# Sixteen experts on all tokens, or on tokens sorted into blocks by group

## The chip, the cores and the metric

The kernel runs on one NeuronCore of a Trainium2 chip. Its engines work in parallel and wait for each other through semaphores: PE (TensorE, matmuls; its weight loads are listed apart as PEld), DVE (VectorE), ACT (ScalarE), POOL (GpSimd), and SP, which here only issues DMAs. The metric is the device time of one execution in microseconds (us), lower is better.

## What is computed

Three layers on 256 tokens of width 1024, all in float32. The first two (a gated delta rule beside a dilated attention, then a convolved gated FFN) and the mixer of the third are the same in both kernels. The change is in the end of the third layer, a mixture of experts with two levels of routing:

```
def hier_moe(h, wg, bg, we, be, w_gate, w_up, w_down):     # h = rms_norm(x, ffn_norm_g)
    glog = t @ wg + bg                                      # 4 groups: the best one (top 1)
    ...
    elog_sel = jnp.einsum('tge,tg->te', elog, g_onehot)     # 4 experts of that group: the best two
    ...
    gates = (g_onehot[:, :, None] * w_local[:, None, :]).reshape(T, N_EXPERTS) * p_group
    for e in range(N_EXPERTS):                              # 16 experts, 1024 -> 256 -> 1024
        hid = jax.nn.silu(t @ w_gate[e]) * (t @ w_up[e])
        y = y + gates[:, e:e + 1] * (hid @ w_down[e])
```

A token's gates are zero in all groups but its own, so at most 4 of the 16 experts can matter to it, and 2 do.

## The kernel before, in words

Weights arrive as tiles of 128 partitions x 1024 float32 (512 KB each). To multiply in float32 precision on the fast path, every tile is split into two float32r parts: ACT copies it rounded (`hi`), DVE subtracts that from the tile (`lo`), and PE makes three products for each operand pair, hi\*hi, hi\*lo and lo\*hi (helper `product`, lines 1246 to 1248). All activations are split in the same way.

A ring of 3 raw slots (`ring`) and 3 split slots (`w`) carries the tiles. SP issues the load of tile n+3 when DVE has made `lo` of tile n; ACT makes `hi` of tile n+3 (line 1586) when PE has finished tile n; DVE makes its `lo` (line 1824); PE waits for `lo`. There are 330 tiles in all, 96 of them of the experts.

The mixture of experts begins after the last token sums of `w_out` (PE). DVE adds them to `x` (line 1032), ACT takes squares and a root, DVE scales the rows, PE turns them (line 1327), ACT and DVE split them into `act`, POOL adds the parts again into `h` (line 2142), and PE makes the router's logits from `h` (lines 592, 594) after the first two expert tiles. DVE then works out the gates in short steps on a few columns each (lines 1046 to 1100); PE turns them and spreads each expert's gate over the partitions (line 629), with ACT copying the results (line 807).

Every expert has four up tiles (two of the gate projection, two of the up projection) and two down tiles. With up tiles the weights stand still in PE (128x128) and all 256 tokens move: 8 x 3 matmuls of 256 columns per tile (`project`). With down tiles the hidden values stand still, and the weights move: 2 token halves x 2 column halves x 3 matmuls of 512 columns per tile (`token_product`). Down tiles of expert e come after the up tiles of expert e+1. ACT makes the silu (line 790), DVE the gated up projection (1110) and the product's `hi` (1118), POOL the product and its `lo` (1199, 1203). The experts run in loops on each engine, and the sums over all experts stay in four PSUM banks until the end, when DVE adds them to `x` (line 1142) and SP stores four parts.

## Time and profile before

| | |
|---|---|
| time, median of 3 runs | 1334.0 us (1331.05 to 1336.51) |
| profiled execution, span | 1334.9 us |
| PE / PEld busy | 1263.1 us (95%) / 1168.5 us (88%) |
| DVE / ACT / POOL busy | 817.3 / 663.9 / 328.5 us |
| DMA | 180.98 MB, mean 136 GB/s |
| mixture of experts, from the addition of the mixer's result (1025.6) to the end | 309.3 us |

The profiled execution's span is within 0.1% of the median, so times read from it need no scaling. A busy time is a sum over instructions; PE's matmuls overlap, so that a matmul lasts longer than the distance to the next one. In rows of matmuls the distance between two starts is what one costs when PE is never idle.

### The profile page before, as it was taken

What the parts mean: (1) busy time and instruction counts of PE and PEld (TensorE: products, weight loads), DVE (VectorE), ACT (ScalarE), POOL (GpSimd) and SP (SyncE); (2) the same over time, 40 slices, a digit from 0 to 9 for tenths busy, and PEclk for the clock granted to TensorE, in tenths of its full rate; (3) what the DMA queues carried; (4) which work ended last, traced back from release to release, by engine and by line L of the source; (5) the groups of instructions that cost most, each with busy time, mean ns of one, the idle gap of its engine ahead of it and who ended that gap; (6) DMA issues with size and microseconds to landing.
All of it is one profiled execution on the core that took longest, in us unless ns stands there. A gap on an engine that the chain in (4) does not pass through costs nothing.

```text
span 1334.9 us, 24113 instructions
## 1 busy us (share of the span) xinstructions
PE 1263.1 (95%) x8802; PEld 1168.5 (88%) x8802; DVE 817.3 (61%) x1293; ACT 663.9 (50%) x1085; POOL 328.5 (25%) x370
## 2 busy tenths in 40 slices
PE   8999898999998999899899999888689999999998
PEld 7998787999997999788899998788668889999997
DVE  5766446766666855655766666597455455555554
ACT  6654245655555763345655555583144444444442
POOL 2013300322222101610322222487200122222221
PEclk9999899999999999899899999998659889999999
DMA  6542003565553444103365556233103245665563
GB/s 225 174 144 94 33 1 110 183 188 186 182 185 124 160 146 143 45 1 98 117 190 183 182 186 190 93 127 111 48 1 111 79 144 186 186 186 182 186 186 127
DMA packets 49788, 180.98 MB, mean 136 GB/s; under 512 B 5568, under 2 KB 5728, under 8 KB 49600
## 3 DMA queue, kind: packets, MB, share of 16 engines
q1 hardware_dynamic: 48816, 176.98, 41.8%
q0 software_dynamic: 912, 3.16, 0.7%
q8 instruction: 42, 0.69, 0.2%
q14 instruction: 18, 0.15, 0.0%
HBM read 179.07 MB, written 1.05 MB: 135 GB/s over the span
## 4 chain that ended last, share of the span: by engine, by line
PE 84%; DVE 6%; POOL 4%; ACT 4%; issue 1%; DMA 0%; POOLq 0%; SPq 0%; DVEq 0%; ACTq 0%
PE bank L1246 23%; PE bank L1247 22%; PE bank L1248 22%; PE bank L1481 2%; PE bank L1470 1%; PE bank L1479 1%; PE bank L1305 1%; PE bank L1327 1%; ACT sq L1595 1%; POOL region L1186 1%; PE bank L1296 1%; PE bank L629 1%; POOL region L1161 1%; POOL region L1164 1%; PE bank L1333 1%
## 5 line engine op out<-in xcount | busy, mean ns | idle before, releaser
L1824 DVE TENSOR_TENSOR w<-ring,w 128x1024 fp32r<-128x1024 f32 x330 | 412.2, 1250 | 220.1 <-ACT w L1586 220.1
L1246 PE MATMUL bank<-act,w 128*128 128x256 f32 x1728 | 499.9, 289 | 15.9 <-DVE w L1824 6.1
L1247 PE MATMUL bank<-act,w 128*128 128x256 f32 x1728 | 494.9, 286 | 0.0
L1248 PE MATMUL bank<-act,w 128*128 128x256 f32 x1728 | 494.7, 286 | 0.0
L1586 ACT ACTIVATE w<-ring 128x1024 fp32r<-128x1024 f32 x330 | 347.7, 1055 | 184.6 <-PE bank L1248 180.0
L1246 PEld LDWEIGHTS bank<-act,w 128*128 128x128 f32 x1728 | 337.9, 196 | 23.1 <-issue 15.4
L1247 PEld LDWEIGHTS bank<-act,w 128*128 128x128 f32 x1728 | 337.9, 196 | 2.3
L1248 PEld LDWEIGHTS bank<-act,w 128*128 128x128 f32 x1728 | 337.4, 195 | 0.0
L2094 DVE SCALAR_TENSOR_TENSOR region<-bank,pf,region 128x255 f32<-128x255 f32 (+1 forms) x176 | 84.8, 482 | 77.3 <-ACT region L1787 66.2
L1246 PE MATMUL bank<-w,hid 128*128 128x512 f32 x304 | 119.3, 392 | 4.1 <-POOL hid L2196 2.1
L1247 PE MATMUL bank<-w,hid 128*128 128x512 f32 x304 | 118.9, 391 | 0.0
L1248 PE MATMUL bank<-w,hid 128*128 128x512 f32 x304 | 118.3, 389 | 0.0
L1787 ACT ACTIVATE region<-bank,pf 128x256 f32<-128x256 f32 x88 | 49.6, 564 | 134.3 <-PE bank L1248 134.3
L2193 POOL TENSOR_TENSOR region<-region 128x256 f32<-128x256 f32 x44 | 65.2, 1482 | 183.0 <-DVE region L2094 133.8
L2142 POOL TENSOR_TENSOR h<-act 128x256 f32<-128x256 f32 x48 | 38.5, 841 | 256.7 <-DVE act L1846 256.6
L1246 PE MATMUL bank<-w,act 128*128 128x256 f32 (+1 forms) x208 | 71.7, 345 | 0.0
L1246 PEld LDWEIGHTS bank<-w,hid 128*128 128x128 f32 x304 | 57.3, 188 | 15.6 <-issue 2.9
L1248 PE MATMUL bank<-w,act 128*128 128x256 f32 (+1 forms) x208 | 69.5, 334 | 0.0
L1247 PE MATMUL bank<-w,act 128*128 128x256 f32 (+1 forms) x208 | 69.4, 334 | 0.0
L1248 PEld LDWEIGHTS bank<-w,hid 128*128 128x128 f32 x304 | 57.1, 188 | 12.4
L1247 PEld LDWEIGHTS bank<-w,hid 128*128 128x128 f32 x304 | 57.3, 189 | 9.7
L1199 POOL TENSOR_TENSOR region<-region 128x256 f32<-128x256 f32 x32 | 24.7, 772 | 154.6 <-DVE region L1110 154.6
(329 smaller groups left out, 1656.8 us busy)
## 6 DMA issues: line engine op xcount, KB each, us to landing
ring<-wtiles SPq DMA_DIRECT2D x330, 512.0 KB, 3.6
region<-packp POOLq DMA_DIRECT2D x4, 512.0 KB, 4.3
cst<-consts SPq DMA_DIRECT2D x1, 1348.0 KB, 11.6
x<-xt SPq DMA_DIRECT2D x2, 512.0 KB, 5.9
out<-x SPq DMA_DIRECT2D x4, 256.0 KB, 2.7
pa<-packa POOLq DMA_DIRECT2D x3, 285.5 KB, 4.6
pb<-packb SPq DMA_DIRECT2D x1, 260.5 KB, 11.5
cst<-consts SPq DMA_DIRECT2D x1, 192.5 KB, 2.7
```

The costliest lines, as they stand in the source:

```text
L629: mm = t.matmul(bank[6 + i % 2][:, j * S:(j + 1) * S], ident[0:NE, 2 * i + j:2 * i + j + 1].to_broadcast([NE, P]), gate_t[0:NE, :], start= ...
L1199: pl.tensor_tensor(e_prod[:, j, :], e_act[:, j, :], e_up[:, j, :], ALU.mult).then_inc(ex_prod, 1)
L1246: t.matmul(out_, still[:, 0], moving[:, 0], start=first, stop=False)
L1247: t.matmul(out_, still[:, 0], moving[:, 1], start=False, stop=False)
L1248: return t.matmul(out_, still[:, 1], moving[:, 0], start=False, stop=last)
L1481: mm = t.matmul(bank[6 + g][:, u % 4 * P:u % 4 * P + P], xs[:, u, :], uinv[:, u, :], start=True, stop=True)
L1586: a.activation(w_hi[:, s, :], ring[:, s, :], ACT.Copy).then_inc(hi_ready, 1)
L1787: a.activation(dst[:, q, :], bank[UP_BANKS[2 * q + w]][:, 0:S], ACT.Identity, scale=pf_("conv", p * 6 + w * 3 + 2), bias=pf_("bias", p * 2 ...
L1824: v.tensor_tensor(w_lo[:, s, :], ring[:, s, :], w_hi[:, s, :].bitcast(F32), ALU.subtract).then_inc(lo_ready, 1)
L2094: ins = v.scalar_tensor_tensor(dst[:, q, j:], src[:, 0:S - j], pf_("conv", p * 6 + w * 3 + 2 - j), dst[:, q, j:], ALU.mult, ALU.add)
L2142: pl.tensor_tensor(h[:, k, :], act_hi[:, k, :].bitcast(F32), act_lo[:, k, :].bitcast(F32), ALU.add).then_inc(h_ready, 1)
L2193: pl.tensor_tensor(glu_p[:, q, :], glu_a[:, q, :], glu_v[:, q, :], ALU.mult).then_inc(prod_done, 1)
```

## The change

The experts run on tokens sorted by group. 640 places, five blocks of 128, are filled with the 256 tokens: the largest group gets blocks 0 and 1, the other three one block each; places without a token stay zero. Two one-hot matrices made on the chip do the sorting: `pm` (token x place) gathers the tokens by matmul, its transpose `pmt` adds the results back to the tokens. The gates are gathered with them. The gain `ffn_norm_g` goes into the router's weights and into the splitting of the gathered columns; the norm's factor goes in with the gates, so that the router starts from `x` itself (transposed by PE, line 1707).

The expert weights are in an array of their own, `etiles`. A group's number is read from the counts into a register of SP (`gid`), and the loads of that group's tiles take their address from it. So no expert tile can be loaded before the routing has counted the groups; the loop of loads of `wtiles` ends with the mixer. Raw slots are five (three of `ring`, two in `sq`), split slots seven (three of `w`, four of `wx`).

Per expert there are still four up tiles and two down tiles of the same size. Now the tokens stand still in all of them and the weights move in 512 columns: an up tile holds two slices of 128 rows by 512 columns (gate 256, up 256). An expert of the first (largest) group is applied to two blocks, one of the others to one block. The order of tiles is as before: up tiles of step i+1, down tiles of step i. After the up tiles the hidden values have tokens on partitions, so PE turns them before the down product (`turn_hidden`). POOL makes `lo` of the first down tile of every expert (`POOL_TILE`), DVE of the other five. Loops are written out on all engines. After a group's last expert its sums leave PSUM, are split (`result_hi`, `result_lo`) and scattered to the tokens (`scatter`).

```diff
+BLOCKS = NG + 1
+PLACES = BLOCKS * P
+UPS, DOWNS = 4, 2
+E_TILES = UPS + DOWNS
+RAWS, WEIGHTS = 5, 7
...
+def blocks_of(p):
+    return (0, 1) if p == 0 else (p + 1,)
...
+def tile_order():
+    out = []
+    for i in range(len(STEPS) + 1):
+        if i < len(STEPS):
+            out += [(*STEPS[i], j) for j in range(UPS)]
+        if i >= 1:
+            out += [(*STEPS[i - 1], j) for j in range(UPS, E_TILES)]
+    return out
...
+POOL_TILE = UPS
...
-            keep_warm(14)
-            turn(2 * DEPTH + 1, SECOND_SUMS)
-            first = T2 + U_EXP
...
+            XT_BANKS = (0, 1, 4, 5)
+            for i in range(2 * NT):
+                c, j = divmod(i, 2)
+                pe.wait_ge(*x_half(i + 1))
+                for k in range(KD // 2):
+                    mm = transpose(bank[XT_BANKS[i]][:, k * P:(k + 1) * P],
+                                   x[:, c, (j * KD // 2 + k) * P:(j * KD // 2 + k + 1) * P])
+                mm.then_inc(xt_turned.sem, 1)
+            pe.wait_ge(*consts_ready(2))
             for c in range(NT):
                 for k in range(KD):
-                    t.matmul(bank[5][:, c * NR:(c + 1) * NR], h[:, k, c * P:(c + 1) * P], pb_("wrt", k * NR, NR),
-                             start=k == 0, stop=False)
-                mm = t.matmul(bank[5][:, c * NR:(c + 1) * NR], ones[0:1, :], pb_("rbias", 0, NR, slice(0, 1)),
-                              start=False, stop=True)
-            mm.then_inc(rt_done, 1)
-            def expert_up(n, e, slots, between=None):
-                for j, s in enumerate(slots):
-                    if j == 2 and between:
-                        between()
-                    if j < 2:
-                        pe.wait_ge(ex_act, 2 * e + j - 1)
-                    else:
-                        pe.wait_ge(ex_up, 2 * e + j - 3)
-                    project(n + j, s, bank[j][:, 0:S])
-            def expert_down(n, e, slots, first=False, last=False):
-                pe.wait_ge(ex_hid, 2 * e + 2 + EX_CREDITS)
-                for j, s in enumerate(slots):
-                    tile_in(n + j)
-                    token_product(EXPERT_SUMS, hid_both[:, :, j, :], s, first and j == 0, last and j == 1)
-            for j in range(2, 4):
-                project(first + j, j % SLOTS, bank[j][:, 0:S])
-            def gates_out():
-                pe.wait_ge(gates_ready, 1)
+                    if k % (KD // 2) == 0:
+                        pe.wait_ge(*(xt_act, xt_dve)[c](k // (KD // 2) + 1))
+                    mm = t.matmul(bank[2][:, c * NR:(c + 1) * NR], x_turned[:, c, k, :], pb_("wrt", k * NR, NR),
+                                  start=k == 0, stop=k == KD - 1)
+            mm.then_inc(rt_done.sem, 1)
+            keep_warm(6)
...
+            def gather(out_, k, first, end):
                 for c in range(NT):
-                    mm = transpose(bank[4][0:NE, c * P:(c + 1) * P], r_gate[:, c, :])
-                mm.then_inc(gt_done, 1)
-                pe.wait_ge(gt_ready, 1)
-                for i in range(NE // 2):
-                    if i >= 2:
-                        pe.wait_ge(gbc_ready, i - 1)
+                    for part in range(2):
+                        mm = t.matmul(out_, x_parts[:, part, c, k * P:(k + 1) * P], pm[:, c, first:end],
+                                      start=c == 0 and part == 0, stop=c == NT - 1 and part == 1)
+                mm.then_inc(ga_done.sem, 1)
+            pe.wait_ge(*xs_lo(NT))
+            pe.wait_ge(*pm_ready(1))
+            for k in range(KD):
+                if k >= 4:
+                    pe.wait_ge(*ga_lo(k - 3))
+                gather(bank[4 + k % 4][:, 0:S], k, 0, S)
+            keep_warm(4)
...
+            def expert_up(i):
+                p, e = STEPS[i]
+                for j in range(UPS):
+                    w_ = weights_in(E_AT[(p, e, j)])
+                    if i == 0:
+                        pe.wait_ge(*ga_lo(2 * j + 2))
+                        if j == UPS - 1:
+                            gather_gates()
+                    for n, b in enumerate(blocks_of(p)):
+                        for kk in range(2):
+                            mm = product(bank[n], act_g[:, :, 2 * j + kk, b * P:(b + 1) * P],
+                                         w_[:, :, kk * 512:(kk + 1) * 512], j == 0 and kk == 0, j == UPS - 1 and kk == 1)
+                    mm.then_inc(e_done.sem, 1)
...
+            def expert_down(i):
+                p, e = STEPS[i]
+                pe.wait_ge(*ex_lo(hidden_count(i)))
+                if i == 0:
+                    pe.wait_ge(*ga_lo(2 * KD))
+                    pe.wait_ge(*pt_ready(3))
+                elif e == 0:
+                    pe.wait_ge(*y_lo(finished(p - 1)))
+                for jj in range(DOWNS):
+                    w_ = weights_in(E_AT[(p, e, UPS + jj)])
+                    for n, b in enumerate(blocks_of(p)):
+                        still = hid_both[:, :, hidden_place(i, n), jj * P:(jj + 1) * P]
+                        for j in range(2):
+                            mm = product(acc_bank(p, n, j), still, w_[:, :, j * HALF:(j + 1) * HALF],
+                                         e == 0 and jj == 0, e == NPG - 1 and jj == DOWNS - 1)
+                            if e == NPG - 1 and jj == DOWNS - 1 and (n, j) != (len(blocks_of(p)) - 1, 1):
+                                mm.then_inc(y_done.sem, 1)
+                    mm.then_inc(e_done.sem, 1)
...
+            def turn_hidden(i):
+                p, e = STEPS[i]
+                for n, b in enumerate(blocks_of(p)):
+                    pe.wait_ge(*ex_hid(hidden_count(i - 1) + n + 1))
+                    for jj in range(DOWNS):
+                        mm = transpose(bank[2 + n if p == 0 else 1][:, jj * P:(jj + 1) * P],
+                                       hidv[:, hidden_place(i, n), jj * P:(jj + 1) * P])
+                    mm.then_inc(ht_done.sem, 1)
...
+            for i in range(NE + 1):
+                if i < NE:
+                    expert_up(i)
+                if i == 0:
+                    pe.wait_ge(*pm_ready(2))
+                    for k in range(KD):
...
+                if i >= NPG and (i - 1) % NPG == 0 and i > 1:
+                    p = (i - 1) // NPG - 1
+                    pe.wait_ge(*y_lo(finished(p)))
                     for j in range(2):
-                        mm = t.matmul(bank[6 + i % 2][:, j * S:(j + 1) * S],
-                                      ident[0:NE, 2 * i + j:2 * i + j + 1].to_broadcast([NE, P]), gate_t[0:NE, :],
-                                      start=True, stop=True)
-                    mm.then_inc(gbc_done, 1)
-            expert_up(first + 4, 1, (1, 2, 0, 1), gates_out)
-            expert_down(first + 8, 0, (2, 0), first=True)
-            with pe.Fori(1, NE - 1) as e:
-                expert_up(e * RING + (first + 4), e + 1, (1, 2, 0, 1))
-                expert_down(e * RING + (first + 8), e, (2, 0))
-            expert_down(first + NE * RING - 2, NE - 1, (1, 2), last=True)
+                        scatter(p, j, p == 0, False)
+                if i >= 1:
+                    expert_down(i - 1)
+                if i < NE:
+                    turn_hidden(i)
+            for j in range(2):
+                pe.wait_ge(*y_lo(finished(NG - 2) + j + 1))
+                scatter(NG - 1, j, False, True)
...
+            def weight_hi(n):
+                act.wait_ge(e_in[n % RAWS], 16 * (n // RAWS + 1))
+                if n >= WEIGHTS:
+                    act.wait_ge(*e_done(n - WEIGHTS + 1))
+                a.activation(weight_slot(n)[:, 0], raw_slot(n), ACT.Copy).then_inc(e_hi.sem, 1)
...
+            def silu(i):
+                p, e = STEPS[i]
+                act.wait_ge(*e_done(E_AT[(p, e, UPS - 1)] + 1))
+                if i == 0:
+                    act.wait_ge(*gs_ready(1))
+                for n, b in enumerate(blocks_of(p)):
+                    a.activation(e_act[:, hidden_place(i, n), :], bank[n][:, 0:S], ACT.Silu,
+                                 scale=gs[:, b, 0:1]).then_inc(ex_act.sem, 1)
...
+            def weight_lo(n):
+                dve.wait_ge(*e_hi(n + 1))
+                w_ = weight_slot(n)
+                v.tensor_tensor(w_[:, 1], raw_slot(n), w_[:, 0].bitcast(F32), ALU.subtract).then_inc(e_lo_dve.sem, 1)
...
+            for n in range(len(E_ORDER) + WEIGHTS + 2):
+                if n < len(E_ORDER) and E_ORDER[n][2] != POOL_TILE:
+                    weight_lo(n)
+                if n == 1:
+                    local_gates()
+                    put_places(S, PLACES)
...
+                pl.tensor_tensor(x_parts[:, 1, c, :], x[:, c, :], x_parts[:, 0, c, :].bitcast(F32), ALU.subtract).then_inc(xs_lo.sem, 1)
+            for n, tile in enumerate(E_ORDER):
+                if tile[2] == POOL_TILE:
+                    pool.wait_ge(*e_hi(n + 1))
+                    w_ = weight_slot(n)
+                    pl.tensor_tensor(w_[:, 1], raw_slot(n), w_[:, 0].bitcast(F32), ALU.subtract).then_inc(e_lo_pool.sem, 1)
...
-            with pool.Fori(0, NE) as e:
-                expert(e)
...
+            for n, (p, e, j) in enumerate(E_ORDER):
+                if group[p] is None:
+                    sp.wait_ge(*gid_ready(min(p, 1) + 1))
+                    group[p] = sp.value_load(gid[0:1, p:p + 1], min_val=0, max_val=NG - 1)
+                if n >= RAWS:
+                    if E_ORDER[n - RAWS][2] == POOL_TILE:
+                        sp.wait_ge(*e_lo_pool(split_by(n - RAWS, True)))
+                    else:
+                        sp.wait_ge(*e_lo_dve(split_by(n - RAWS, False)))
+                sp.dma_start(raw_slot(n), etiles[bass.ds(group[p], 1), e * E_TILES + j].rearrange("o p n -> (o p) n")
+                             ).then_inc(e_in[n % RAWS], 16)
```

Three places of the instruction order, as they stand in the program. First, PE from the end of `w_out` on, before: keep_warm is line 1313, the turned rows are `y`, and the expert's first tile follows at once.

```order
L1246 MATMUL bank<-w,act 128x512
L1247 MATMUL bank<-w,act 128x512
L1248 MATMUL bank<-w,act 128x512
L1313 MATMUL bank<-cst 128x128 x14
L1327 MATMUL bank<-cst,y 128x128 x8
L1313 MATMUL bank<-cst 128x128 x4
L1327 MATMUL bank<-cst,y 128x128 x8
L1246 MATMUL bank<-act,w 128x256
```

The same place now (keep_warm is line 1693, the gather line 791, `x` is turned by line 1707):

```order
L1707 MATMUL bank<-cst,x 128x128 x16
L773 MATMUL bank<-pb,h 128x20 x16
L1693 MATMUL bank<-cst 128x128 x6
L780 MATMUL bank<-region,cst 128x4
L781 MATMUL bank<-region,cst 128x4
L782 MATMUL bank<-region 128x4
L783 MATMUL bank<-region,cst 128x4
L784 MATMUL bank<-region 128x4
L1693 MATMUL bank<-cst 128x128 x8
L791 MATMUL bank<-pm,act 128x256 x32
L1693 MATMUL bank<-cst 128x128 x4
L1626 MATMUL bank<-w,act_g 128x512
```

The router, the counts and the gather of the first two blocks have moved ahead of the first expert tile. Second, DVE from the token sums to the first `lo` of an expert's weights, before (1846 splits `act`, 1046 to 1077 are the router's steps):

```order
L1032 TENSOR_TENSOR x<-x,bank 128x1024 x2
L1838 RECIPROCAL x_inv<-x_rms 128x1
L1840 TENSOR_SCALAR y<-x,x_inv 128x1024
...
L1846 SCALAR_TENSOR_TENSOR act<-bank,pb,act 128x256 x8
L1824 TENSOR_TENSOR w<-ring,w 128x1024 x3
L1061 COPY region<-bank 128x40
L1046 TENSOR_REDUCE region<-region 128x2
```

and now (1404 writes `pm`, 1415 splits a gathered slice, 1431 to 1440 work out the experts' scores, 1421 makes `lo` of a weight tile, 1445 begins the gates):

```order
L1404 TENSOR_SCALAR pm<-region 128x256 x2
L1408 SCALAR_TENSOR_TENSOR gid<-cst,region 128x3
L1410 TENSOR_TENSOR region<-region 128x8
L1415 SCALAR_TENSOR_TENSOR act_g<-bank,pb,act_g 128x256 x8
L1431 TENSOR_TENSOR region<-region 128x16 x2
L1433 TENSOR_REDUCE region<-region 128x8
...
L1440 TENSOR_TENSOR region<-region 128x2
L1421 TENSOR_TENSOR w<-ring,w 128x1024 x2
L1445 TENSOR_REDUCE region<-region 128x2
```

The router's first choice, `pm`, the gathered slices and the scores have moved ahead of the first weight tile; the gates stand between the second and the third. Third, DVE in the loop over experts, before (one pass), register instructions left out:

```order
L1824 TENSOR_TENSOR w<-ring,w 128x1024
...
L1110 TENSOR_TENSOR region<-bank,region 128x256
...
L1824 TENSOR_TENSOR w<-ring,w 128x1024
...
L1118 TENSOR_TENSOR hid<-region 128x256 x2
...
L1824 TENSOR_TENSOR w<-ring,w 128x1024
```

and an expert of the second group now, with five tiles on DVE (1471 is the gated product, 1480 the `lo` of the turned hidden values):

```order
L1471 SCALAR_TENSOR_TENSOR mix<-bank,region 128x256
L1421 TENSOR_TENSOR wx<-sq,wx 128x1024
L1480 TENSOR_TENSOR hid<-bank,hid 128x256
L1421 TENSOR_TENSOR wx<-ring,wx 128x1024 x2
L1421 TENSOR_TENSOR w<-ring,w 128x1024
L1421 TENSOR_TENSOR w<-sq,w 128x1024
L1471 SCALAR_TENSOR_TENSOR mix<-bank,region 128x256
```

The number of tiles per expert on DVE went from six to five, the four short instructions to two that read PSUM, and the sixth tile stands in POOL's row of work (`L1572 TENSOR_TENSOR`), where the short products stood.

## Rows read from the trace of the kernel before

**Rows 1.** Windows of the expert part: stretch, length, busy of each engine, PEclk, DMA share, GB/s

```profile
1025.60:1034.20 8.60, 6.43 (x54) 5.92 (x53) 4.77 (x9) 5.05 (x10) 0.03 (x1) 1.00 0.24 74
1034.20:1077.00 42.80, 40.19 (x239) 36.36 (x239) 18.12 (x51) 20.31 (x32) 9.62 (x14) 0.80 0.18 62
1077.00:1317.00 240.00, 240.00 (x1699) 226.59 (x1700) 132.48 (x143) 114.18 (x126) 54.92 (x57) 1.00 0.60 187
1317.00:1334.90 17.90, 12.03 (x55) 9.40 (x54) 6.78 (x10) 2.12 (x2) 2.02 (x3) 1.00 0.20 71
```

**Rows 2.** PE in order of time: start us, us, instruction

```profile
1008.20 0.39 PE L1246 MATMUL bank<-w,act 128*128 128x512 f32 x1
1008.43 0.39 PE L1247 MATMUL bank<-w,act 128*128 128x512 f32 x1
...
1034.43 0.28 PE L1247 MATMUL bank<-act,w 128*128 128x256 f32 x1
1034.55 0.28 PE L1248 MATMUL bank<-act,w 128*128 128x256 f32 x1
...
1040.82 1.96 PE L592 MATMUL bank<-pb,h 128*128 128x20 f32 x16 [0.59 <-POOL h L2142]
```

**Rows 3.** Groups by form, 1075 to 1325 us: count, busy, mean ns, idle before

```profile
L1824 DVE TENSOR_TENSOR w<-ring,w 128x1024 fp32r<-128x1024 f32 x89 | 113.9, 1280 | 94.6 <-ACT w L1586 94.6
L1586 ACT ACTIVATE w<-ring 128x1024 fp32r<-128x1024 f32 x89 | 94.1, 1058 | 98.1 <-PE bank L1248 93.9 <-DMA ring<-wtiles 4.2
L1110 DVE TENSOR_TENSOR region<-bank,region 128x256 f32<-128x256 f32 x30 | 12.8, 426 | 11.9 <-PE bank L1248 11.9
```

**Rows 4.** Groups by form of DVE and POOL, whole span

```profile
L1846 DVE SCALAR_TENSOR_TENSOR act<-bank,pb,act 128x256 fp32r<-128x256 f32 x8 | 3.7, 484 | 2.0 <-ACT act L1606 1.7
L1142 DVE TENSOR_TENSOR x<-x,bank 128x512 f32<-128x512 f32 x4 | 2.7, 687 | 4.9 <-PE bank L1248 4.9
L2171 POOL TENSOR_TENSOR y<-region,cst 128x1024 f32<-128x1024 f32 x12 | 24.8, 2074 | 39.4 <-DVE region L2043 26.5 <-PE bank L1470 12.9
L2196 POOL TENSOR_TENSOR hid<-region,hid 128x256 fp32r<-128x256 f32 x44 | 32.5, 738 | 79.3 <-DVE hid L2104 79.1
```

**Rows 5.** POOL beside DVE, in order of time

```profile
1103.15 2.33 POOL L1203 TENSOR_TENSOR hid<-region,hid 128x256 fp32r<-128x256 f32 x2 [4.65 <-DVE hid L1118]
...
1103.75 1.23 DVE L1824 TENSOR_TENSOR w<-ring,w 128x1024 fp32r<-128x1024 f32 x1 [0.41 <-ACT w L1586]
...
125.39 4.54 POOL L2171 TENSOR_TENSOR y<-region,cst 128x512 f32<-128x512 f32 x3
...
126.51 1.56 DVE L2035 TENSOR_TENSOR region<-cst,y 128x512 f32<-128x512 f32 x1 [0.20 <-POOL y L2171]
```

**Rows 6.** ACT and DVE at the norm and the router, in order of time

```profile
1029.51 1.04 ACT L1595 ACTIVATE sq<-x 128x1024 f32<-128x1024 f32 x1
...
1040.88 1.28 ACT L790 ACT_TABLE_LOAD   x1 [2.84 <-POOL credit L1190]
...
1046.12 0.16 DVE L1046 TENSOR_REDUCE region<-region 128x2 f32<-128x8 f32 x1
1046.32 0.17 DVE L1048 TENSOR_TENSOR region<-region 128x8 f32<-128x8 f32 x1
```

**Rows 7.** DMA issues (the page): KB each, us from issue to landing

```profile
ring<-wtiles SPq DMA_DIRECT2D x330, 512.0 KB, 3.6
out<-x SPq DMA_DIRECT2D x4, 256.0 KB, 2.7
```

**Rows 8.** Windows of the first loads and of two stretches at the lower clock

```profile
6.00:14.00 8.00, 7.43 (x61) 7.24 (x60) 3.08 (x6) 7.57 (x11) 0.00 (x0) 1.00 1.03 424
945.00:1000.00 55.00, 47.30 (x248) 38.49 (x250) 31.40 (x84) 20.73 (x60) 0.00 (x0) 0.56 0.09 29
1062.00:1076.00 14.00, 12.85 (x42) 10.43 (x42) 2.84 (x5) 6.62 (x11) 2.98 (x4) 0.51 0.01 1
1076.00:1080.00 4.00, 3.63 (x31) 3.45 (x30) 3.52 (x4) 1.79 (x2) 1.48 (x1) 1.00 0.46 136
```

533 lines of the change are left out of this document (369 added, 164 removed).

## The prediction, made before the changed kernel was run

> **What bounds the kernel now.** I read the windows of the expert part first, then PE in order of time, then the groups by form of DVE, ACT and POOL with what ended their idle time. From 1077 to 1317 us PE has 240.00 of 240.00 us busy at the full granted clock [rows 1], and ACT's wait ahead of a weight tile is for PE, 93.9 of 98.1 us [rows 3]. So PE sets the pace there: 0.23 us from one matmul of 512 columns to the next and 0.12 for 256 columns [rows 2], which is 24 x 0.118 = 2.8 us for an up tile and 12 x 0.2275 = 2.7 for a down tile, 16.8 us per expert. Loads fill 0.60 of the DMA engines' time [rows 1]. Around that stand 8.6 us of norm and 42.8 us with the router in them [rows 1]. From the addition of the mixer's result at 1025.6 to the end are 309.3 us, the sum of the four windows. All ahead of 1025.6 stays as it is, so I rebuild only what follows it. The profiled span, 1334.9, is within 0.1% of the median 1334.0, and I use the one for the other.
>
> **The change, part by part.** What it removes: PE had 96 matmuls of 256 columns and 24 of 512 per expert. It will have 72 of 512 for an expert of the first group (two blocks) and 36 for the others: 36 x 0.2275 = 8.2 us. With the hidden values' turning (two of 128 columns, 0.26) that is 8.45. What it does not remove: every one of the 96 tiles is still loaded and split. A split takes 1.06 us of ACT and 1.23 to 1.28 of DVE, I take 1.25 [rows 3, 5]. So where PE's work halves, I must look who is next.
>
> (a) To the first expert product. DVE adds four halves, 4 x 0.69 = 2.8 us [rows 4]. PE turns the last half (0.5), DVE copies two (2 x 0.69), and the router's 16 matmuls take 2 x 1.96 = 3.9 [rows 2]: at 8.6 us. Seven DVE steps of 0.2 from start to start [rows 6] pick the group (1.4), PE counts (0.3), and some nine more steps with two of `pm` give places (1.8): 12.1. The other chain, ACT's squares and root (1.04 and half a microsecond of small steps after the last half [rows 6]), two copies of x and two subtractions on POOL, ends by 10.2 and lies beside it. Gathering eight slices goes at 0.5 us each, DVE's 0.48 being the slowest link [rows 4], with 1.2 for the first: 5.2. Then fifteen DVE steps for the scores, 3.0, and the first `lo`, 1.25. PE starts at 21.5. The loads are hidden there: the group number is ready about 11, the first tile, 3.6 us later [rows 7] plus a register load, by 17.
>
> (b) The first four up tiles. Behind the second `lo` DVE has eleven gate steps (2.2) and two of `pm` (1.0), so the third is 5.7 us behind the first; then PE has two tiles of 2.73 and the gates' gather (1.2): 12.4.
>
> (c) The rest of the gather. Copy of the gates 0.4, ACT's table load (1.3 [rows 6]) and two silus 2.1, DVE's gated product 1.0, eight slices of 384 columns on DVE at 0.6, between the 0.48 of 256 columns and 1.5 times that (4.8), turning `pm` and the hidden values with ACT's copies 2.9: 11.2.
>
> (d) PE alone, the first group's other 20 tiles and four up tiles of the next: 20 x 2.73 + 4 x 1.36 + turning 1.6 = 61.6. DVE and ACT have 16 us per expert here and are no limit.
>
> (e) The last 68 tiles, 11.33 experts. This decides the case. PE alone: 11.33 x 8.45 + 32 scatter products (7.3) = 103. DVE: 5 x 1.25 + 0.48 + 0.43 = 7.16 per expert [rows 3, 4]. The sixth tile is POOL's. No row shows POOL subtracting 1024 columns into the rounded type. A multiply of 1024 takes 2.07 us, the subtraction of 256 takes 0.74 [rows 4]; four of those would be 2.95. I take 2.4, nearer to the row of the same size. But POOL and DVE get in each other's way: two POOL subtractions (1.48 us at 0.74 each) took 2.33 beside a `lo` of 1.23 [rows 5], and a DVE multiply of 512 columns took 1.56 beside POOL's 1024 columns, against 0.69 for such an add from PSUM [rows 4, 5]. That looks like one running and the other standing. With that, DVE and POOL do one tile after the other: 7.16 + 2.4 = 9.56 per expert, above PE's 8.45. 11.33 x 9.56 = 108.4, with four result copies of groups two and three (2.7) 111.1.
>
> The Trainium skill ("SBUF — State Buffer", Who interferes with whom) says that a DVE instruction with two SBUF inputs and a GpSimd one that reads SBUF share a port that is locked for a whole instruction. The trace agrees, with the 2.33 and the 1.56 above. By that rule a POOL tile costs DVE its length once, which is the 9.56; if instead both slow each other in proportion, it is the third rival below.
>
> (f) The end: last matmul 0.4, rounding copy 0.6, subtraction 0.7, four scatter products 0.9, two additions 1.4 [rows 4], issue 0.6, landing of the store 2.7 [rows 7]: 7.3.
>
> (g) Clock. In (a) PE has little to do. After the spreading matmuls of before the granted clock stood at 0.51 for 14 us [rows 8], and was 1.00 again once the products ran. The first product tile then costs 12 x 0.43 = 5.1 instead of 2.7, and a little is lost behind (c): 3.3.
>
> Sum: 21.5 + 12.4 + 11.2 + 61.6 + 111.1 + 7.3 + 3.3 = 228.4, against 309.3. 1025.6 + 228.4 = 1254.0 us.
>
> **The rivals.**
>
> *PE keeps the pace (1246 us).* POOL's tile finds DVE idle, as DVE has 5 tiles to do in PE's 8.45. Then (e) is 103. For it: seven split slots let DVE run ahead. Against: DVE and POOL together need more than PE, and a lead is eaten in a few experts.
>
> *Raw slots come back late (1279 us).* The load of tile n+5 waits for `lo` of tile n, and SP's loads behind it wait too. For POOL's tile that circle is rounding copy 1.06 + POOL + 0.1 + load 3.6 [rows 7], then one more tile's data before the next circle begins. The first loads moved 424 GB/s at a full DMA share [rows 8], 1.24 us per tile; 187 GB/s at 0.60 [rows 1] would mean 1.7. With 1.3 an expert takes 6.1 + POOL's time. At 2.4 that is 8.5, just at PE's pace. It decides from a POOL tile of 3.5 us on. If POOL is slowed in proportion (the later one of the pair: 2.33 - 0.74 = 1.6 for 0.74, 2.2 times, and more beside a `lo` that never pauses; I take 2.4), 2.4 becomes 5.8 and an expert 11.9: 135 + 1, 25 more than in (e).
>
> *Data rate.* If a tile takes 1.7 us of the DMA engines, 68 take 116, and the sum is 1259. It is inside the range of the forecast, and I keep it there.
>
> *The clock falls in the last three groups.* Low clock means 0.43 per product: 36 x 0.43 + 0.5 = 16 us per expert, 196 in (e), and the whole gain is gone: 1339. If it holds in a third of the time it costs 28, 1282. For it: 945 to 1000 us ran at 0.56 with PE busy in 47.3 of 55 us [rows 8], so gaps between products matter. Against: from 1076 on it was full as soon as 512 and 256 column products came in a row, and in (e) PE would idle only 1.1 of 9.6 us; at the low clock it has no idle left. The side of "slower" is this mechanism and no other: it needs the low clock all through (e), and any of it in (d), where low means 57 more.
>
> The Trainium skill ("TensorE: Matmul & The Clock Gate", HAM oscillation — how this bites in real kernels) warns of just this form: 128 rows of tokens per weight tile, and between the tiles waits for loads in which the clock falls again for every tile. The row above that would show it, 945 to 1000, has small matmuls, so no run here shows it for tiles of this size yet.
>
> *The start is longer.* (a) to (c) are chains of short steps with 45 us in all. If semaphores and register loads make them half as long again, 22 more, 1276. The group sizes change addresses only, not the amount of work, so the sorting can't fail to save the products.
>
> **How the numbers follow.** Chances: port as in (e) 0.45 (1245 to 1265), PE's pace 0.12, late slots 0.18, clock in part 0.10, clock all through 0.04, longer start 0.08, something faster than all of this 0.03. The likeliest is 1254. The range 1238 to 1286 leaves out the full clock case and the ends of the others. Slower by over 0.5% is the clock all through, 0.04; within 0.5% 0.01; faster 0.95. (0.5%, 7 us, is about what a measurement of this kernel can tell.)
>
> **What would show it.** Right: first product of `act_g` and `w` about 1047 to 1050; group one's tiles at 2.7 us; in the last three groups 9.3 to 9.9 us per expert, PE busy below 95%, DVE's mean for `lo` longer than 1.28 in front of or behind POOL's tile, POOL's tile 2.4 to 3.2 us; PEclk 1.00 there. If POOL's tile is 5 us or ACT waits mostly for `ring<-etiles`, the late slots are right. If PE has no idle time at 0.2275 per product, PE's pace is. If PEclk is below 0.9 after 1140, the clock is. I am wrong altogether if the part ahead of 1025.6 changes by more than 2 us.

## The result, and the profile after

The changed kernel takes 1254.13 us (median of 4 runs, 1253.56 to 1258.28), the kernel before 1335.17 beside it: a ratio of 0.94, with a 95% interval of 0.9381 to 0.9419. 1254.0 was predicted. The profiled execution is the longest of the four (1258.28, span 1256.5); the spans of the others are 1251.8 to 1252.4, so the stages below hold about 4 us that the median does not. The total was right and most terms were near; the reason given for the largest of them was not.

Windows of the changed kernel over what was 309.3 us in [rows 1] (columns as there), cut at round times. The events themselves: first addition of the mixer's result at 1024.98, gather at 1042.63, first expert product at 1051.51, first up tile of the second expert at 1074.83, PE's turn of the fifth expert's hidden values (the first expert of the second group) at 1137.06, last product at 1248.77:

```profile
1025.60:1047.00 21.40, 19.00 (x130) 18.42 (x129) 13.60 (x34) 8.96 (x17) 4.66 (x2) 0.76 0.29 106
1047.00:1060.00 13.00, 9.02 (x35) 7.10 (x35) 12.41 (x37) 8.93 (x12) 0.00 (x0) 0.87 0.51 165
1060.00:1071.00 11.00, 9.99 (x59) 8.85 (x58) 6.21 (x9) 6.64 (x10) 2.40 (x1) 1.00 0.85 315
1071.00:1133.00 62.00, 62.00 (x288) 51.37 (x287) 33.07 (x40) 32.70 (x46) 7.21 (x3) 1.00 0.53 167
1133.00:1245.00 112.00, 107.71 (x471) 85.06 (x469) 81.72 (x83) 76.75 (x94) 29.25 (x12) 1.00 0.83 288
1245.00:1256.50 11.50, 5.37 (x22) 3.60 (x20) 4.29 (x7) 1.58 (x3) 0.00 (x0) 0.90 0.27 91
```

The whole first group runs with PE busy without a gap, as in [rows 1]. In the last three groups PE has 4.3 us of gaps in 112 at a full clock, and the DMA share has risen from 0.60 to 0.83. The groups by form of that stretch, 1133 to 1245 us (the first is DVE's, the others are all of ACT's on weight tiles):

```profile
L1421 DVE TENSOR_TENSOR wx<-ring,wx 128x1024 fp32r<-128x1024 f32 x18 | 25.2, 1412 | 8.0 <-ACT wx L1071 7.9
L1071 ACT ACTIVATE wx<-ring 128x1024 fp32r<-128x1024 f32 x21 | 22.3, 1061 | 7.7 <-DMA ring<-etiles 7.5
...
L1071 ACT ACTIVATE w<-ring 128x1024 fp32r<-128x1024 f32 x17 | 17.8, 1066 | 7.0 <-DMA ring<-etiles 6.2 <-PE bank L1628 0.3
...
L1071 ACT ACTIVATE wx<-sq 128x1024 fp32r<-128x1024 f32 x16 | 17.1, 1066 | 9.2 <-PE bank L1628 4.8 <-DMA sq<-etiles 4.3
L1071 ACT ACTIVATE w<-sq 128x1024 fp32r<-128x1024 f32 x10 | 10.6, 1062 | 5.3 <-DMA sq<-etiles 5.0 <-PE bank L1628 0.3
```

In [rows 3] ACT waited for PE ahead of a weight tile. Now 23.0 of ACT's 29.2 us of idle time there are waits for a load: that is what the prediction named as the mark of the late raw slots. DVE waits for ACT, as it did before. And the transfers take longer (DMA issues of the page, columns as in [rows 7]):

```profile
ring<-wtiles SPq DMA_DIRECT2D x234, 512.0 KB, 3.5
ring<-etiles SPq DMA_DIRECT2D x58, 512.0 KB, 5.0
sq<-etiles SPq DMA_DIRECT2D x38, 512.0 KB, 4.7
```

One expert in order of time (POOL, DVE and ACT of the changed kernel, each apart):

```profile
1167.76 2.40 POOL L1572 TENSOR_TENSOR w<-ring,w 128x1024 fp32r<-128x1024 f32 x1 [8.45 <-ACT w L1071]
1177.31 2.40 POOL L1572 TENSOR_TENSOR w<-ring,w 128x1024 fp32r<-128x1024 f32 x1 [7.14 <-ACT w L1071]
...
1168.90 2.35 DVE L1421 TENSOR_TENSOR w<-ring,w 128x1024 fp32r<-128x1024 f32 x1 [2.02 <-ACT w L1071]
1171.17 0.41 DVE L1480 TENSOR_TENSOR hid<-bank,hid 128x256 fp32r<-128x256 f32 x1
1171.51 1.21 DVE L1421 TENSOR_TENSOR wx<-ring,wx 128x1024 fp32r<-128x1024 f32 x1
1172.64 2.35 DVE L1421 TENSOR_TENSOR wx<-sq,wx 128x1024 fp32r<-128x1024 f32 x2
...
1170.30 1.06 ACT L1071 ACTIVATE wx<-sq 128x1024 fp32r<-128x1024 f32 x1 [0.19 <-DMA sq<-etiles]
1171.53 1.06 ACT L1071 ACTIVATE wx<-sq 128x1024 fp32r<-128x1024 f32 x1 [0.17 <-DMA sq<-etiles]
1173.81 1.07 ACT L1071 ACTIVATE wx<-ring 128x1024 fp32r<-128x1024 f32 x1 [1.22 <-DMA ring<-etiles]
1174.78 0.46 ACT L1083 ACTIVATE region<-bank,region 128x256 f32<-128x256 f32 x1
1176.17 2.26 ACT L1071 ACTIVATE w<-ring 128x1024 fp32r<-128x1024 f32 x2 [0.93 <-DMA ring<-etiles]
```

From POOL tile to POOL tile are 9.55 us here (9.5 to 10.0 for the experts without a scatter after them, about 10.4 with one), where 9.56 were predicted, but they can be added up from other parts. POOL's tile n ends at 1170.16; the load that waited for its slot (tile n+5) has landed at 1173.81, 3.65 later; the next one, POOL's own next tile, at 1176.17, 2.36 later; ACT's copy and the hand-over take 1.14: 2.40 + 3.65 + 2.36 + 1.14 = 9.55. The lock is there too: DVE's `lo` at 1168.90 begins while POOL has 1.26 us to go and takes 2.35 in place of 1.22. It frees the slot of POOL's next tile only at 1171.25, 4.92 ahead of that landing.

So the same 9.55 can be added up in a second way, with the lock in it: from POOL's start to the end of DVE's `lo` 3.49 (2.40 of POOL, 1.09 behind it), 4.92 from there to the landing of POOL's next tile, 1.14 to POOL. The loads ahead of these two land 1.23 us apart (ACT at 1170.30 and 1171.53), these two 2.36. Without the 1.09 the sum would be 8.46, if the landing came earlier by as much. Which of the two sums is the true one this trace does not say.

### The profile page after: what moved, and what is told of

It reads as the page before. It is cut to its first block, busy times and chain, and to the rows that moved or that the text cites. A ratio compares the mean times of both kernels' runs of the same rounds, so it can differ in the third digit from the quotient of the medians.

```text
span 1256.5 us, 21300 instructions
## 1 busy us (share of the span) xinstructions
PE 1173.9 (93%) x7748; PEld 1059.7 (84%) x7748; DVE 805.2 (64%) x1292; ACT 657.2 (52%) x1095; POOL 306.7 (24%) x315
## 4 chain that ended last, share of the span: by engine, by line
PE 75%; DVE 10%; ACT 5%; DMA 4%; POOL 4%; issue 1%; SPq 0%; DVEq 0%; POOLq 0%; ACTq 0%
PE bank L1626 19%; PE bank L1627 19%; PE bank L1628 19%; DMA ring<-etiles 2%; PE bank L1861 2%; PE bank L1707 2%; PE bank L1859 2%; PE bank L1850 2%; DVE wx L1421 1%; DVE w L1421 1%; PE bank L1685 1%; DMA sq<-etiles 1%; POOL region L1560 1%; POOL y L2551 1%; PE bank L1676 1%
## 5 line engine op out<-in xcount | busy, mean ns | idle before, releaser
L2204 DVE TENSOR_TENSOR w<-ring,w 128x1024 fp32r<-128x1024 f32 x234 | 289.0, 1236 | 122.3 <-ACT w L1966 122.3
L1626 PE MATMUL bank<-act,w 128*128 128x256 f32 x1216 | 353.0, 290 | 13.6 <-DVE w L2204 5.8
L1627 PE MATMUL bank<-act,w 128*128 128x256 f32 x1216 | 348.4, 286 | 0.0
L1628 PE MATMUL bank<-act,w 128*128 128x256 f32 x1216 | 347.9, 286 | 0.0
L1966 ACT ACTIVATE w<-ring 128x1024 fp32r<-128x1024 f32 x234 | 246.2, 1054 | 79.2 <-PE bank L1628 79.1
L1626 PEld LDWEIGHTS bank<-act,w 128*128 128x128 f32 x1216 | 237.5, 195 | 19.2 <-issue 14.3
L1627 PEld LDWEIGHTS bank<-act,w 128*128 128x128 f32 x1216 | 237.9, 196 | 2.0
L1628 PEld LDWEIGHTS bank<-act,w 128*128 128x128 f32 x1216 | 237.5, 195 | 0.0
L2573 POOL TENSOR_TENSOR region<-region 128x256 f32<-128x256 f32 x44 | 65.2, 1481 | 183.2 <-DVE region L2474 124.9
L1626 PE MATMUL bank<-w,hid 128*128 128x512 f32 x214 | 84.9, 397 | 2.0 <-POOL hid L2576 2.0
L1627 PE MATMUL bank<-w,hid 128*128 128x512 f32 x214 | 84.5, 395 | 0.0
L1628 PE MATMUL bank<-w,hid 128*128 128x512 f32 x214 | 84.2, 394 | 0.0
L2522 POOL TENSOR_TENSOR h<-act 128x256 f32<-128x256 f32 x40 | 32.0, 840 | 167.1 <-DVE act L2226 167.1
L2576 POOL TENSOR_TENSOR hid<-region,hid 128x256 fp32r<-128x256 f32 x44 | 32.7, 743 | 81.0 <-DVE hid L2484 80.8
L1626 PEld LDWEIGHTS bank<-w,hid 128*128 128x128 f32 x214 | 40.3, 188 | 10.5 <-issue 2.8
L2536 POOL TENSOR_TENSOR h<-h,cst 128x256 f32<-128x256 f32 x16 | 10.7, 672 | 156.3 <-PE bank L1767 156.3
L1628 PEld LDWEIGHTS bank<-w,hid 128*128 128x128 f32 x214 | 40.2, 188 | 9.8
```

What stands on the lines that cost most here:

```text
L1626: t.matmul(out_, still[:, 0], moving[:, 0], start=first, stop=False)
L1627: t.matmul(out_, still[:, 0], moving[:, 1], start=False, stop=False)
L1628: return t.matmul(out_, still[:, 1], moving[:, 0], start=False, stop=last)
L1966: a.activation(w_hi[:, s, :], ring[:, s, :], ACT.Copy).then_inc(hi_ready, 1)
L2204: v.tensor_tensor(w_lo[:, s, :], ring[:, s, :], w_hi[:, s, :].bitcast(F32), ALU.subtract).then_inc(lo_ready, 1)
L2522: pl.tensor_tensor(h[:, k, :], act_hi[:, k, :].bitcast(F32), act_lo[:, k, :].bitcast(F32), ALU.add).then_inc(h_ready, 1)
```

## The experiments

In the table that follows the experiments, the stages of each are given from its first addition of the mixer's result; "low clock" is the time at the lower clock (1.2 GHz) from there to the first up tile of the second expert, added up from the clock's record. "Last 68" is term (e), from PE's turn of the fifth expert's hidden values to the last product; "fifth turn" is when that turn starts.

Two cautions on single traces. The part ahead of the first addition is the same in all of them, and yet that addition stands anywhere from 1022.1 to 1027.1 us, which the medians have in them and the stages do not. And the six versions whose start has the same instructions as the changed kernel (the changed kernel and experiments 1, 2, 3, 5, 6) have their gather at 16.1 to 17.7 us and their low clock at 13.7 to 17.1; in experiment 4, with shorter loads, it is 20.5. So a difference in the start of about 1.6 us, or of 3.4 us of low clock, is not yet a difference between two versions. The last 68 tiles vary far less: 105.70 or 105.71 in each of the six versions where PE alone sets their pace.

**1. Two raw slots more** (`raws7`), in columns of `mix` that are free by then and in a new buffer:

```diff
-RAWS, WEIGHTS = 5, 7
+RAWS, WEIGHTS = 7, 7
+        more = sb("more", 1024)
...
+            if i == 5:
+                return mix[:, 4:8, :].rearrange("p k s -> p (k s)")
+            if i == 6:
+                return more[:]
```

> Seven raw slots instead of five (two more in memory that is free by then); all else as in the changed kernel. Theory P (one port): in the last three groups DVE's five subtractions and POOL's one exclude each other, 9.5 to 10 us per expert, and slots do not matter: 1254, at most 2 us less. Rival R (slots): the load of tile n+5 waits for POOL's tile n and lands 4.8 us later, and this circle sets the pace: with seven slots it goes at PE's 8.45 us per expert, 8 us less, 1246.

1250.46 us (1247.38 to 1251.55), ratio 0.9357 (0.9341 to 0.9372). The last 68 tiles take 105.7 us in place of 111.7. The 1246 of the rival was too low, as it took PE's pace for 8.45 us per expert: from turn to turn PE takes 8.5 to 8.6 us here, and 10.4 where a scatter comes in between, 9.33 on the mean. The window of the 68 tiles in its trace:

```profile
1136.37:1242.07 105.70, 104.77 (x464) 84.62 (x463) 83.77 (x82) 76.53 (x94) 28.86 (x11) 1.00 0.80 284
```

and ACT's and DVE's largest groups by form, 1135 to 1240 us:

```profile
L1076 ACT ACTIVATE w<-ring 128x1024 fp32r<-128x1024 f32 x27 | 28.4, 1063 | 4.8 <-PE bank L1633 4.3
...
L1426 DVE TENSOR_TENSOR w<-ring,w 128x1024 fp32r<-128x1024 f32 x22 | 30.1, 1395 | 5.0 <-ACT w L1076 4.9
```

ACT waits for PE again, and PE is busy in 104.8 of 105.7. DVE's `lo` still takes 1.40 us on the mean where 1.22 is its own time, so DVE and POOL still stand in each other's way, and it costs nothing that the 105.7 show.

**2. One raw slot more** (`raws6`: `RAWS = 6`, the rest as in 1):

> One raw slot more than the changed kernel, six in place of five. Circle theory: with five slots the interval from POOL tile to POOL tile is POOL 2.40, landing of the load that waited for it 3.65, one more tile until POOL's own 2.36, ACT's copy and hand-over 1.14, in all 9.55 us. With six slots the load that waits for POOL's tile is that of POOL's next tile itself, or of its neighbour: 2.40 + 3.65 to 5.0 + 1.14 = 7.2 to 8.5 us, less than PE's 9.33, so the last groups fall to 105.7 to 106.5 us and the time to 1250 to 1252, as with seven. Port theory (DVE and POOL one after the other, whatever the slots): 111.7 us and 1254 stay.

1250.67 us (1248.81 to 1252.52), ratio 0.9352 (0.9336 to 0.9368); the last 68 tiles take 107.1. One slot gives back 4.6 of the 6.0 us. ACT's waits for loads add up to 4.9 us in 1133 to 1235. The lock is as before (DVE's `lo` from `sq` takes 1.51 us on the mean), and 4.6 us are gone all the same.

**3. No tile for POOL** (`alldve`: `POOL_TILE = -1`), five slots:

> DVE makes all six lo parts of an expert, POOL none; five raw slots as before. P: DVE then needs 6 x 1.23 + 0.9 + 0.3 = 8.6 us per expert without any waiting for the port, PE with scattering 9.1: 5 to 8 us less than the changed kernel, 1247, although an engine has more work. R: the same gain, since POOL's 2.4 us leave the circle. If a second engine were a help as its work suggests (a third rival, W), DVE would be the limit at 8.6 + nothing gained: no change or slower, 1254 to 1262.

1251.95 us (1251.0 to 1256.44), ratio 0.9387 (0.9368 to 0.9405); the last 68 tiles take 106.1 in the profiled run. The median is not told apart from the changed kernel's by their intervals; the trace is. This alone doesn't tell the two reasons apart, since it takes away both the lock and POOL's 2.40 us in the circle.

**4. Half of each load** (`half`). This leaves out the loads' second 512 columns of every expert tile; the work on the tiles is the same.

```diff
-sp.dma_start(raw_slot(n), etiles[bass.ds(group[p], 1), e * E_TILES + j].rearrange("o p n -> (o p) n")
+sp.dma_start(raw_slot(n)[:, 0:512], etiles[bass.ds(group[p], 1), e * E_TILES + j, :, 0:512].rearrange("o p n -> (o p) n")
```

> Only the first 512 columns of each expert tile are loaded (the other half of the slot keeps what was in it, so the output is not the reference's); splits and products keep their size. P: no change in the last three groups, 1254 (1252 to 1256), ACT's waits for loads shrink. R: a load lands in 3.6 us or less instead of 4.8, the circle shortens by 1.2 us per expert, 6 to 8 us less, 1247. If the data rate were the limit: also 8 less.

1250.86 us (1249.09 to 1254.27), ratio 0.9369 (0.935 to 0.9389). That interval overlaps the changed kernel's (0.9381 to 0.9419) a little, so the reading rests on the trace, where the last 68 tiles take 107.0. The page:

```profile
ring<-etiles SPq DMA_DIRECT2D x58, 256.0 KB, 2.8
```

The loads land in 2.8 us in place of 5.0, and with POOL's tile and DVE untouched the 111.7 become 107.0. Had DVE and POOL one after the other set the pace, this would have changed nothing.

**5. Seven slots and no tile for POOL** (`raws7_dve`):

> Seven raw slots and all six weight lo's on DVE: both releases of the last groups at once. If PE's own pace is all that is left in raws7 (PE 104.5 busy of 106), this gives the same 105 to 106 us in the last groups and 1250 to 1252. If what was left is POOL's tile beside DVE, the last groups fall to 103 and the time to 1248. If DVE with six tiles (6 x 1.23 + 0.9 = 8.3 us per expert, more with the scores) becomes late at the rounds with scores, it rises to 107 to 108.

1252.5 us (1248.02 to 1253.18), ratio 0.9366 (0.9346 to 0.9386), the last 68 tiles 105.7 to the hundredth as in 1. So once the slots are there the lock costs nothing in these tiles; 105.7 is PE's own pace.

**6. More use of the port** (`raws7_port`), seven slots, and two more POOL instructions behind each of POOL's tiles, whose result nobody reads:

```diff
...
+            port_ops = 0
...
                     pl.tensor_tensor(w_[:, 1], raw_slot(n), w_[:, 0].bitcast(F32), ALU.subtract).then_inc(e_lo_pool.sem, 1)
+                    for _ in range(2):
+                        if port_ops:
+                            pool.wait_ge(port_done, port_ops)
+                        port_ops += 1
+                        pl.tensor_tensor(mix[:, 2:4, :].rearrange("p k s -> p (k s)"), cst[:, 0:512], cst[:, 512:1024], ALU.mult).then_inc(port_done, 1)
```

> Seven raw slots as in raws7, and two more POOL multiplications of 128x512 from one SBUF tile into unused columns behind each POOL tile (some 1.2 us each, from the 2.40 us of the 128x1024 tile); nobody waits for them, they take no slot, and only POOL's own next tile stands behind them. Theory P (an SBUF-to-SBUF instruction of POOL and a two-input SBUF one of DVE exclude each other): DVE and POOL want 5 x 1.23 + 2.4 + 2.4 = 10.95 us of the port per expert, more than the 9.33 us of raws7, so the last groups take 11.33 x 10.95 + 2.7 = 127 us in place of 105.7, and the time is 1268 to 1273. Theory R (only the slots were short, the port costs nothing): 105.7 us and 1250.5. Single weight lo instructions of DVE beside POOL should stand at 2.2 to 2.4 us in P and at 1.23 in R.

1259.76 us (1259.56 to 1260.3), ratio 0.9437 (0.9421 to 0.9452), 9 us above experiment 1, whose interval ends at 0.9372; the last 68 tiles take 117.2. So the lock has a price, once there is enough work for it: POOL itself was idle for 41 us ahead of its tiles, so it was not late by its own work. Its window of the 68 tiles:

```profile
1132.83:1250.06 117.23, 107.25 (x465) 85.51 (x463) 100.77 (x83) 76.51 (x94) 73.60 (x34) 0.99 0.73 256
```

the groups by form of the two kinds of instruction in it:

```profile
L1427 DVE TENSOR_TENSOR w<-ring,w 128x1024 fp32r<-128x1024 f32 x22 | 37.9, 1750 | 2.0 <-ACT w L1077 2.0
...
L1584 POOL TENSOR_TENSOR mix<-cst 128x512 f32<-128x512 f32 x23 | 45.4, 1976 | 0.9
```

and DVE's steps that read PSUM beside POOL, in order of time:

```profile
1176.97 3.67 POOL L1584 TENSOR_TENSOR mix<-cst 128x512 f32<-128x512 f32 x2
1178.03 0.41 DVE L1486 TENSOR_TENSOR hid<-bank,hid 128x256 fp32r<-128x256 f32 x1
1178.36 1.27 DVE L1495 TENSOR_TENSOR y_parts<-bank,y_parts 128x512 fp32r<-128x512 f32 x2
```

The 127 us expected were too many, in part because I counted 1.23 us for a `lo`. That is its duration; from one to the next on DVE are 1.13 (two in 2.35 in the row at 1172.64). And DVE is some tiles ahead of PE when the 68 begin: 52 of its `lo` stand in the window, not 57. With 52 x 1.13 for DVE, 11 x 2.40 for POOL's tiles and 23 x 1.2 for the extra ones (1.2 is half of 2.40, an estimate; the shortest in the trace took 1.27) the port has about 113 us of work in 117.2: nearly full. By the same count the changed kernel has 5 x 1.13 + 2.40 = 8.05 us of it per expert, less than the 8.5 to 8.6 of PE without a scatter.

Part of the 11.5 us is the clock's. It was granted in full but for 3.4 us from 1165.7 on, right behind a gap of PE of 3.0 us; behind the other gap of that length, at 1208, it stayed full:

```profile
1165.54 0.56 PE L1719 MATMUL bank<-cst,mix 128*128 128x128 f32 x2 [3.01 <-DVE mix L1477]
...
1166.32 0.63 PE L1639 MATMUL bank<-wx,act_g 128*128 128x512 f32 x1
1166.75 0.63 PE L1640 MATMUL bank<-wx,act_g 128*128 128x512 f32 x1
```

Eight products at 0.43 us in place of 0.23 are 1.6 us, an estimate of the most that this can have cost.

**7. POOL's `x_lo` later** (`xlo_later`), in the start. In the changed kernel a step of two instructions in DVE's routing chain takes 3.72 us, ten times its own 0.36 (POOL, DVE and PE in order of time):

```profile
1031.97 4.66 POOL L1567 TENSOR_TENSOR act<-x,act 128x1024 fp32r<-128x1024 f32 x2 [23.11 <-ACT act L1059]
...
1032.93 3.72 DVE L1370 SCALAR_TENSOR_TENSOR region<-region,cst 128x4 f32<-128x4 f32 x2
...
1039.25 3.62 PE L1693 MATMUL bank<-cst 128*128 128x128 f32 x16
...
1042.63 4.01 PE L791 MATMUL bank<-pm,act 128*128 128x256 f32 x32
...
1051.51 0.50 PE L1626 MATMUL bank<-w,act_g 128*128 128x512 f32 x1 [3.98 <-DVE w L1421]
```

The change:

```diff
+            pool.wait_ge(*oh_ready(1))
             for c in range(NT):
                 pool.wait_ge(*xs_hi(c + 1))
```

> POOL's two subtractions for the gathered tokens wait until the group's one-hot is made, and all else stays. P: the step of 3.72 us on DVE (two small operations with both inputs in SBUF, line 1370) waits for POOL's port; now it takes 0.4, the group number, pm and the gather come 3.4 us earlier, limited by POOL's end at 1038.8 instead of 1042.6: 3 to 4 us less, 1250.5. Rival: the long step has another reason (its form, its place in the program): it stays 3.7 us, 1254.

1256.23 us (1255.01 to 1258.58), ratio 0.9413 (0.9398 to 0.9429): no gain, where 3 to 4 us were expected. In its trace the step takes its own time, and the next one with two inputs from SBUF stands in its place:

```profile
1031.04 0.36 DVE L1370 SCALAR_TENSOR_TENSOR region<-region,cst 128x4 f32<-128x4 f32 x2
...
1034.27 2.29 DVE L1387 SCALAR_TENSOR_TENSOR region<-cst,region 128x4 f32<-128x4 f32 x1
```

So the long step goes with POOL's instruction and not with its own form or place. The gather starts 2.5 us earlier and the first product 1.4, the end stands 1.4 us nearer to the first addition, and the low clock lasts 3.4 us longer; these are not far beyond what the same start shows by itself (gather at 16.1 and first product at 25.6 in experiment 6, for 15.2 and 25.2 here).

**8. `x_lo` on DVE** (`raws7_x`), on top of experiment 1: both subtractions ahead of DVE's routing chain, ACT's copies of `x` ahead of its squares.

```diff
...
+            for c in range(NT):
+                dve.wait_ge(*xs_hi(c + 1))
+                v.tensor_tensor(x_parts[:, 1, c, :], x[:, c, :], x_parts[:, 0, c, :].bitcast(F32), ALU.subtract).then_inc(xs_lo.sem, 1)
...
-            for c in range(NT):
-                pool.wait_ge(*xs_hi(c + 1))
-                pl.tensor_tensor(x_parts[:, 1, c, :], x[:, c, :], x_parts[:, 0, c, :].bitcast(F32), ALU.subtract).then_inc(xs_lo.sem, 1)
```

> raws7, with the two x lo subtractions of the start on DVE in place of POOL, ahead of the routing chain, and ACT's x hi copies ahead of its squares. Theory P: no instruction of the routing chain then stands beside POOL, so the 3.72 us step and the 2.29 us one both fall to about 0.36; two DVE subtractions of 1.2 us come in, and the gather starts at 13.7 to 15 us from the first x addition in place of 17.65. If the low clock takes it back as in xlo_later, the first expert product is at 25 and the time is as raws7 or 1 to 2 us more; if not, the first product is at 23 and the time 1247 to 1248. Theory without a port: the steps keep 3.72 us, or the two subtractions only add 2.4 us: 1252 to 1253.

1248.63 us (1246.08 to 1251.6), ratio 0.9355 (0.9338 to 0.9373). Although DVE has 2.35 us more to do, the gather starts 4.3 us earlier than in 1, beyond the spread of the same start; the steps take 0.36 and 0.22. In the traces the end comes 3.5 us sooner from the first addition; the medians alone don't show it.

**9. Scores and gates behind the first tiles** (`raws7_start`), on top of 8 (ACT's exponentials move in the same way):

```diff
-            local_scores()
...
-                if n == 1:
+                if n == 3:
+                    local_scores()
                     local_gates()
...
-                        if j == UPS - 1:
-                            gather_gates()
...
+                if i == 0:
+                    gather_gates()
```

> raws7_x, and the scores of the first block's own routing, the gates' exponentials of ACT and the gather of the gates moved from ahead of the first expert products to behind the fourth weight tile. Expected: DVE's first weight lo some 2.6 us earlier, the first product at 21 to 23 us from the first x addition, 2 to 3 us less than raws7_x: 1245 to 1247. Against it: PE's work up to the fourth tile is then bound by the weights' landing or by the clock (low until some us after the work gets dense): then the first product is earlier and the fourth tile's is not, and the time equals raws7_x.

1246.48 us (1242.63 to 1247.79), ratio 0.9328 (0.931 to 0.9347). The first product comes 0.8 us earlier than in 8, the fifth expert's turn 1.8, though the gather, whose own chain is unchanged, stands 1.3 us later (14.6 for 13.3). That is no more than one start differs from the next, and the intervals of 8 and 9 overlap: a gain over 8 is likely, not shown.

**10. Less filler ahead of the gather** (`start_short`: `keep_warm(8)` becomes `keep_warm(3)`, on top of 9):

> raws7_start with the filler products between the counting products and the gather cut from 8 to 3. In raws7_start's trace the eight stand from 1037.11 to 1040.54 and the gather's one-hot matrix is ready at 1038.65, so the gather waits 1.7 us for work that nobody reads. If latency decides: gather at 13.0 us from the first x addition in place of 14.59, every later stage 1.5 us earlier, 1244.5 to 1245.5. If the clock decides: the gather and the first weight tiles' products run longer at 1.2 GHz (low clock from 6.83 to 10 us, 3.4 more), a low stretch of 3.4 us full of products costs 1.7 us, and the time is that of raws7_start, 1246 to 1247.

1243.94 us (1242.02 to 1247.29), ratio 0.9323 (0.9305 to 0.9341). The gather starts 1.3 us earlier but takes 5.94 us in place of 4.04, and the first product comes 0.6 later than in 9. The best median of all, but by its interval and its stages the same as 9. The 1.3 us are what the gather of 9 differs by from that of 8 with the same code.

**11. No filler at all** (`start_nowarm`): the 18 filler products between router and first expert product are out.

> raws7_start with all 18 filler products of the stretch between router and first expert product taken out. Latency theory: as with the shorter filler, gather at about 13 us from the first x addition, 1244 to 1246. Clock theory: PE is idle for some 2 us twice and for 3 us before the first product, the clock is at 1.2 GHz for 5 to 12 us more with the gather and the first products in it, which costs half of that, 3 to 6 us: 1247 to 1251. Low clock ahead of the first up tile of the second expert: 6.83 us in raws7_start, 12 to 19 here by the clock theory.

1246.36 us (1245.35 to 1249.25), ratio 0.9338 (0.9323 to 0.9354). PE in its trace:

```profile
1036.51 6.24 PE L794 MATMUL bank<-pm,act 128*128 128x256 f32 x32 [1.54 <-DVE pm L1413]
1045.52 0.80 PE L1632 MATMUL bank<-w,act_g 128*128 128x512 f32 x1 [2.77 <-DVE w L1430]
...
1047.82 0.63 PE L1634 MATMUL bank<-w,act_g 128*128 128x512 f32 x1
1048.25 0.63 PE L1632 MATMUL bank<-w,act_g 128*128 128x512 f32 x1
```

The gather starts 2 us earlier than in 9 and takes 2.2 longer, and the first products are 0.43 us apart. From the first addition to the fifth expert's turn it takes 3.2 us more than 9. The median, though, is that of 9, so this cost stands on the stages of one execution each; and experiment 4, with all its filler, has 20.5 us of low clock as well. That the filler is worth having is not shown.

| us from the first addition | gather | first product | second expert's up | fifth turn | last 68 | low clock |
|---|---|---|---|---|---|---|
| changed kernel | 17.65 | 26.5 | 49.9 | 112.1 | 111.7 | 13.7 |
| 1 `raws7` | 17.7 | 26.6 | 48.7 | 110.9 | 105.7 | 13.7 |
| 2 `raws6` | 17.7 | 26.6 | 49.3 | 111.5 | 107.1 | 17.1 |
| 3 `alldve` | 17.7 | 26.5 | 48.6 | 110.9 | 106.1 | 13.7 |
| 4 `half` | 17.7 | 27.6 | 50.8 | 113.1 | 107.0 | 20.5 |
| 5 `raws7_dve` | 17.7 | 26.5 | 48.6 | 110.8 | 105.7 | 13.7 |
| 6 `raws7_port` | 16.1 | 25.6 | 48.5 | 110.7 | 117.2 | 13.7 |
| 7 `xlo_later` | 15.2 | 25.2 | 48.4 | 110.7 | 111.8 | 17.1 |
| 8 `raws7_x` | 13.3 | 22.2 | 45.1 | 107.4 | 105.7 | 10.2 |
| 9 `raws7_start` | 14.6 | 21.4 | 43.3 | 105.6 | 105.7 | 6.8 |
| 10 `start_short` | 13.3 | 22.0 | 43.9 | 106.1 | 105.7 | 10.2 |
| 11 `start_nowarm` | 12.6 | 21.6 | 46.5 | 108.7 | 105.7 | 20.5 |

## Why the prediction was right, and where its reason was not

**(a) to the first product: 26.5 for 21.5.** The step that failed is "two subtractions on POOL, ends by 10.2 and lies beside it". It lies beside it in time, but locks the port: the step at 1032.93 takes 3.72 us in place of 0.36. I had counted the lock against the weight tiles only. With the lock gone the gather comes 4.3 us (8) and 3.1 us (9) earlier than in 1. The filler ahead of the gather ends at 1042.6, when `pm` has been there since 1040.8; I had it at nothing. The two, 3.4 and 1.8, are about the 5 us that (a) was short of.

The Trainium skill ("SBUF — State Buffer", Who interferes with whom) says that the lock is for a whole instruction and that a DVE instruction with at most one SBUF input, outside DVE's two-port modes, is free of it. The traces agree in both: instructions of 4 columns wait 1 to 2 us for POOL's of 1024 (2.29 for 0.22 in experiment 7), and `hid<-bank,hid` keeps its 0.41 us beside POOL in experiment 6.

**(b), (c) and (g), to the second expert's up tile: 23.3 for 26.9** (49.85 - 26.53; 12.4 + 11.2 + 3.3, and part of the clock's 3.3 lies in (a)). DVE's gathered slices take 0.62 us each where 0.6 was predicted. The sum hides two errors. The first four up tiles with the gates' gather took 15.0 us (1051.51 to 1066.55) for 12.4 and part of (g); the gates' gather in it 2.15 for 1.2. The rest of the gather, (c), took 8.3 for 11.2: the turning, 2.9 of the sum, lies beside DVE's slices and costs nothing.

```profile
1069.83 4.99 DVE L1415 SCALAR_TENSOR_TENSOR act_g<-bank,pb,act_g 128x384 fp32r<-128x384 f32 x8
...
1073.38 1.25 PE L1707 MATMUL bank<-cst,pm 128*128 128x128 f32 x10
```

**(d) 62.2 for 61.6.** PE alone, as said; from 1091 to 1133 its products are 0.232 us apart where 0.2275 was taken.

**(e) 111.7 for 111.1, for another reason.** The step that failed is "DVE and POOL do one tile after the other: 7.16 + 2.4". With the work of both engines and the lock left as they were, more slots (1, 2) or shorter loads (4) made the tiles faster, so this is not what sets the pace.

Its pieces: POOL's tile is 2.40 as estimated, and the lock is real (6). (The 1.56 us of DVE in [rows 5] began beside a POOL instruction of 512 columns, as the row has it, not of 1024 as the prediction says; it is a sign of the lock all the same.) But 1.25 us for a `lo` is a duration, and the next one starts 1.13 after it, just as I had allowed for with PE and not with DVE; and the steps that read PSUM are no part of the lock. The port has 8.05 us to do per expert, PE 8.6 without a scatter and 9.33 on the mean.

What set the pace is the circle of the raw slots, my second rival, at 9.55 for the 8.5 that I gave it: the landings took 3.65 us and 2.36 for the next, for 3.6 and 1.3. One slot more (2), shorter loads (4) or POOL out of the circle (3) each took away 4.6 to 5.6 us, with the slots alone 6.0 (1), where the lock stayed. That the two reasons gave the same number is luck. How much of the 9.55 is the 1.13 us by which the lock delays DVE's `lo` at 1168.90, whose slot is POOL's next, was not separated, and it can be all that the circle has above PE's own 8.6: the 2.36 would then be 1.3 and the delay. So the lock may well have its part in the loss, through the slots and not as work that fills the port. Five slots with POOL's tile and no lock beside it were not run.

**PE's own pace** is 105.7, where the rival had 103. In the last three groups the products are a little farther apart: over the 393 intervals below 0.35 us between recorded expert products the mean is 0.2346 us, against 0.2279 over 322 between products of 512 columns from 1077 to 1317 in the kernel before. 408 x 0.0067 = 2.7. Why they are farther apart is open. Five intervals of the last tile, 1.17 us:

```profile
1247.60 0.40 PE L1626 MATMUL bank<-wx,hid 128*128 128x512 f32 x1
...
1248.77 0.40 PE L1628 MATMUL bank<-wx,hid 128*128 128x512 f32 x1
```

**(f) 7.7 for 7.3**: from the last product at 1248.77 to the end.

**The clock** was 1.00 all through (d) and (e), with gaps of PE of up to 1.5 us in (e), so the rival of 1339 did not come in. The Trainium skill ("TensorE: Matmul & The Clock Gate", HAM oscillation) warned of it for 128 rows of tokens per weight tile, where PE waits for a load between tiles; in this case it did not fall, with 4.3 us of gaps in the 112. In experiment 6 it fell once. In the start it did count, 13.7 us of low clock for the "little to do" of (g); that experiments 7, 10 and 11 gave back to it what they gained in latency fits their traces, but the same start varies by as much.

**The data rate** (1.7 us per tile) is no bound: in experiment 1 105.7 / 68 = 1.55 us per tile at a DMA share of 0.80.

## What to carry to other kernels

When two reasons give the same number, say which experiment parts them: here a slot more for the loads, and more load on the port. And look whether both can be one: the lock can lengthen the circle. For a ring of buffers count the whole circle (user, landing at the DMA share that the new pace will have, the next landing, hand-over), and give it one buffer more than that comes to (here the sixth slot gave 4.6 us, the seventh 1.4). Take rates from the distance between starts on every engine, durations only for what others wait for; and look for the port's lock at every instruction with two SBUF inputs that runs beside POOL, the shortest in a chain of latency first.

## What the runs showed of the hardware that I had not expected

A DVE instruction of 4 columns took 3.72 us for two (2.29 us for one in experiment 7) beside POOL's of 1024 columns. A 512 KB load took 3.5 us from issue to landing (median) ahead of the experts and 5.0 in the experts' stretch, at a DMA share of 0.80, and 2.8 for half of it; 3.6 was the median of the kernel before, whose experts ran at a share of 0.60. The same instructions in the start ran with 13.7 us of low clock in one execution and 17.1 in another, and the gather moved by 1.6 us between them and a third. After a gap of PE of 3.0 us in the midst of dense products the granted clock fell to half for 3.4 us once, and once it did not (6).

The best versions, experiments 9 and 10, stand at a ratio of 0.9328 (0.931 to 0.9347) and 0.9323 (0.9305 to 0.9341) to the kernel before. What bounds them is PE, busy in 104.8 of the 105.7 us of the last 68 tiles.
